# Output bias added to x by GpSimd instead of by two extra matmuls per block

## Chip, cores and metric

One Trainium2 chip (trn2), eight cores, one sequence of the batch on each; all cores run the same program on their own data and exchange nothing. The time is that of the slowest core, in microseconds on the device. Before: 2028.34 us, the median of three runs (2024.27 to 2031.74).

## What is computed

A hybrid encoder block on x of 4096 x 1024 per core. Cut to what matters here:

```python
h = rms_norm(x, g_mix)
u = h @ w_in + b_in                          # GLU | q | k | v
y_conv = silu(layer_norm(depthwise_conv(glu(u)) ...))
y_attn = windowed_gqa_with_sink(rope(q), rope(k), v)
x = x + (concat(y_conv, y_attn) @ w_out + b_out)     # the bias b_out
x = x + memory_cross_attention(rms_norm(x), rms_norm(mem))
x = x + swiglu(rms_norm(x), w_gate, w_up, w_down)
return rms_norm(x, g_final)
```

## The kernel before, in words

The program is written as a list of operations. Each is given to an engine with what it reads and writes (`Sched.op`, L63); `arrange` (L101) then orders the whole list with a cost for each operation: at each step the operation that comes first in the program among those ready takes its engine. `finalize` adds the semaphore waits. Each engine runs its operations in that fixed order, so one that waits holds up all behind it. For GpSimd ("pool") these are one-column powers for the norms (L392 and L1009) and the issue of transfers that convert weights from f32 to bf16.

The first 450 us (stages A and conv) project all blocks of 128 tokens and run the convolution; their results go to scratch in HBM. The rest runs over 8 groups of four blocks. `p_chains(g)` is the front half of a group: LayerNorm and swish of the conv half (`ln_stat`, `ln_z`, `ln_tr`, `ln_silu` with L1042, L1044 and L1046), attention per block (`scores` L1071 and L1075, `smax` L1089, `exps` L1105, `den2` with eight L1125), output projection (`out_proj`), cross attention (`mem_chain`) and the norm before the feed forward. `f_steps(g)` is the feed forward, mostly matmuls of L365 and L1430, whose results VectorE takes from PSUM with L1401, L1407 and L1441. The front half of group g+1 is interleaved with the feed forward of group g, and with `final_steps(g-1)`: the last norm (L386, L392, L1349) and the stores of the output.

The residual x of a block lies in one of two sets of four f32 tiles, `xres[g % 2]`. `xload(t)` (L995) loads x of block t into its tile with a transfer on the SP queue; from group 2 on it is placed behind the store of the block that held the tile. `out_proj` calls `proj` (L1179) with `bias` true: the first of nine matmuls for each half of 512 columns multiplies `ones_pad`, which has ones in row 0 and zeros below, with `bout_pad`, which has b_out in row 0 and zeros below. The sum in PSUM is added to x by VectorE in `resid` (L1196). The tile `bout_pad` is cleared by VectorE (L471) and its row 0 is loaded (L478) on GpSimd's queue. PSUM tiles are handed out from lists, `bank_f` for the feed forward and `bank_p` for the front half; a matmul into a tile waits until the last reader of it is done. `conv_win` (L444) shares each conversion of w_in among VectorE (640 columns, L451), ScalarE and GpSimd (576 columns, L455).

Of the kernel before, what the change touches and what calls it, by code (L numbers as in the profile page):

```python
# [8 lines left out]
ALU = mybir.AluOpType  # L9

P = 128
# [222 lines left out]
def build_program():  # L234
    nc = bass.Bass("TRN2", target_bir_lowering=False)
    sc = Sched(nc)

    def dram_in(name, shape, dt=F32):
        return nc.dram_tensor(name, list(shape), dt, kind="ExternalInput").ap()
# [12 lines left out]
    b_out_d = dram_in("b_out", [D])  # L252
# [21 lines left out]
    def sb(name, shape, dt):  # L274
        return nc.alloc_sbuf_tensor(name, list(shape), dt)

    ident = sb("ident", [P, P], BF16)
    ones_pad = sb("ones_pad", [P, P], BF16)
    bout_pad = sb("bout_pad", [P, D], BF16)
# [15 lines left out]
    cb2 = Buf()  # L295
# [4 lines left out]
    def view(off, nkb, dt, shape):  # L300
        ap = arena[:, int(off * 512):int((off + nkb) * 512)]
        if dt == F32:
            ap = ap.bitcast(F32)
        n = 1
        for s_ in shape:
            n *= s_
        return fit(ap[:, 0:n], shape)
# [4 lines left out]
    def fresh(off, nkb):  # L312
        a = Atom()
        for b_ in atoms[int(off * 2):int((off + nkb) * 2)]:
            a.r.extend(b_.w)
            a.r.extend(b_.r)
        a.r = sorted(set(a.r), key=lambda z: z.n)
        return Buf([a])
# [21 lines left out]
    def bank_p():  # L340
        return free_p.pop(0)
# [7 lines left out]
    def dma(e, out, in_, reads, writes, sem, after=()):  # L349
        eng = {"sp": nc.sync, "act": nc.scalar, "pool": nc.gpsimd}[e]  # L350
        n = 1
        for s_ in in_.shape:
            n *= s_
        n *= 2 if in_.dtype == BF16 else 4
        return sc.op(e, lambda: eng.dma_start(out=out, in_=in_), reads=reads, writes=writes, dma=sem, nbytes=n, after=after)  # L355
# [112 lines left out]
    sc.op("dve", lambda: nc.vector.memset(mhalf[:], -0.5), writes=[cb2])  # L468
    sc.op("dve", lambda: nc.vector.memset(ones_pad[:], 0.0), writes=[cb2])
    sc.op("dve", lambda: nc.vector.memset(ones_pad[0:1, :], 1.0), writes=[cb2])  # L470
    sc.op("dve", lambda: nc.vector.memset(bout_pad[:], 0.0), writes=[cb2])  # L471
    sc.op("dve", lambda: nc.vector.memset(bpad, 0.0), writes=[bpad_b])
    sc.op("dve", lambda: nc.vector.memset(zt, 0.0), writes=[zt_b])
    i2 = dma("pool", mask[:], mask_d, [], [], csem2)
    bisem = DmaSem(nc, "bi")
    dma("pool", bpad[0:1, :], b_in_d.unsqueeze(0), [], [bpad_b], bisem)
    bosem = DmaSem(nc, "bo")
    dma("pool", bout_pad[0:1, :], b_out_d.unsqueeze(0), [], [cb2], bosem)  # L478
    id_b = Buf()
    id_b.atoms[0].w = (i1, i2)  # L480
    cb.atoms[0].w = (c1, c2)
# [281 lines left out]
    for e in range(8):  # L763
# [3 lines left out]
        for c0 in range(0, 64, 12):  # L767
# [3 lines left out]
            def f(e=e, c0=c0, n=n, bk=bk, ta=ta):  # L771
                ins = None
                for k in range(n):
# [3 lines left out]
            o = sc.op("pe", f, reads=[tb_] + [v_[1] for v_ in vws], writes=[bkb], cost=0.1 * n)  # L777
# [5 lines left out]
                  reads=[bkb, gfin_b], writes=[yb], cost=0.1 + 0.05 * n)  # L783
# [11 lines left out]
    def mk(off, nkb, dt, *shape):  # L795
        return view(off, nkb, dt, shape), fresh(off, nkb)
# [4 lines left out]
    WK, _ = mk(137, 16, BF16, KC, D)  # L801
    WK_b = [fresh(137 + 2 * k, 2) for k in range(KC)]
    VW = view(153, 16, BF16, (KC, D))
    VW_b = [reg(153 + 2 * k, 2, BF16, D)[1] for k in range(KC)]
    flags = {}

    def note(*key):
        flags[key] = flags.get(key, 0) + 1

    WO = view(121, 16, BF16, (KC, D))  # L810
    WO_b = reg(121, 16, BF16, D)[1]
# [112 lines left out]
    ymixT = view(169, 8, BF16, (KC, T))  # L924
    ymc_b = [fresh(169 + c, 1) for c in range(4)]
    yma_b = [fresh(173, 4) for _ in range(4)]
# [56 lines left out]
    def p_chains(g, last_f=None):  # L983
        chains = []
        xs = xres[g % 2]
# [9 lines left out]
        def xload(t):  # L995
            def f():
                b = 4 * g + t
                dma("sp", xs[t][0], x_d[b * P:(b + 1) * P, :], [], [xs[t][1]], xres_sem[g % 2][t])
                note("x", g, t)
            return f  # L1000

# [174 lines left out]
            add(t0 + 12.6, pv, banks_free(1))  # L1176
            add(t0 + 13.4, pv_ev)

        def proj(t, weights, wbufs, lhs, lhsb, bias):  # L1179
            out = []  # L1180
            for u in range(2):
                bk, bkb = bank_p()
                pairs = [(lhs(k), weights[:, k, u * 512:(u + 1) * 512]) for k in range(KC)]
                rd = list(lhsb) + list(wbufs)
                if bias:
                    pairs = [(ones_pad[:], bout_pad[:, u * 512:(u + 1) * 512])] + pairs
                    rd = rd + [cb2]
                sc.op("pe", mm_group(bk[:], pairs), reads=rd, writes=[bkb], cost=pe_cost(len(pairs), 512))
                out.append((bk, bkb))
            return out  # L1190
# [9 lines left out]
        def out_proj(t, t0):  # L1200
            st = {}

            def a():
                st["b"] = proj(t, WO, [WO_b], lambda k: ymixT[:, k, t * P:(t + 1) * P], ymc_b + [yma_b[t]], True)

            def b():
                resid(t, st["b"])
            add(t0, a, banks_free(2), seen("ln", g), seen("wo"))
            add(t0 + 1.8, b, seen("x", g, t))
# [35 lines left out]
        def mem_chain(t, t0):  # L1245
            st = {}
            ha, hb = hTm[t % 2]
            pa, pb = Pm[t % 2]
            pta, ptb = PmT[t % 2]
# [6 lines left out]
            norm_chain(t, t0 - 4, ev_m, lambda: flags.get(("att", g), 0) >= 4 and (t < 2 or flags.get(("mc", g, t - 2), 0) >= 1))  # L1256

            def s_mm():
                st["s"] = proj(t, WK, WK_b, lambda k: ha[:, k, :], [hb], False)

            def s_max():
                for u in range(2):
# [27 lines left out]
                give_p(bk, bkb)  # L1290

            def o_mm():
                st["o"] = proj(t, VW, VW_b, lambda k: pta[:, k, :], [ptb], False)
                note("mc", g, t)

            def o_ev():
# [262 lines left out]
```

How the kernel before makes its waits and increments, by code:

```python
    def finalize(self):  # L136
# [58 lines left out]
        cnt = {e: 0 for e in self.ENG}  # L195
        for o in self.ops:
            if o.dma is None and o.signal:
                cnt[o.e] += 1
                rank[(o.e, o.idx)] = cnt[o.e]
        nw = 0
        for o in self.ops:
            eng = self.eng[o.e]
            for k, v in o.waits:
                if isinstance(k, str):
                    eng.wait_ge(self.sems[k], rank[(k, v)])
                else:
                    eng.wait_ge(k.sem, v)
                nw += 1
            ins = o.fn()
            if o.dma is not None:
                ins.then_inc(o.dma.sem, 16)
            elif o.signal:
                ins.then_inc(self.sems[o.e], 1)
        self.stats = dict(n_ops=len(self.ops), n_waits=nw, signals=cnt, end=max(o.start for o in self.ops))
# [1 line left out]
    def final_wait(self, e, dsems):  # L216
        eng = self.eng[e]
        for ds in dsems:
            if ds.count > 0:
                eng.wait_ge(ds.sem, ds.count)
```

## Time and profile before

| | |
|---|---|
| profiled execution | 2019.87 us |
| its span on the slowest core (core 3) | 2018.6 us |
| spans of the eight cores | 1975.7 to 2018.6 us |
| granted TensorE clock, mean of core 3 | 0.959 |
| TensorE, VectorE, ScalarE, GpSimd busy | 92%, 55%, 43%, 6% |
| instructions on GpSimd | 206 |

The profile is of one execution. PE is TensorE's matmuls, PEld its weight loads, DVE VectorE, ACT ScalarE, POOL GpSimd, SP the SyncE queue that issues most loads. L365 is line 365 of the kernel; it is a helper, and stands for most matmul groups. "arena" is the one large SBUF tensor in which nearly all tiles are views. Matmuls are pipelined: a row's duration is longer than the distance to the next one, and it is the distance that counts.

### The profile page before, as it was taken

To read this page: it belongs to the slowest core of one execution; us is meant where nothing else is said; L and a number is where in the kernel's file an instruction comes from. 1 tells how busy PE (TensorE), PEld (TensorE's weight loads), DVE (VectorE), ACT (ScalarE), POOL (GpSimd) and SP (SyncE) were. 2 spreads that over 40 slices of the span, in tenths; PEclk is the share of its full clock that TensorE was granted. 3 is DMA by queue.
4 is the path that set the end of the run, shared out by engine and by line. 5 is a ranking of instruction groups with operands and counts; after the bars stand their busy time and mean duration, and the time that the engine had idled before them with its cause. 6 is when DMAs were issued, how large, how long until landed. Compare 5 with 4: busy or idle time off the path is not lost.

```text
span 2018.6 us, 34398 instructions; the slowest of 8 cores (1975.7 to 2018.6 us)
## 1 busy us (share of the span) xinstructions
PE 1854.5 (92%) x11516; PEld 970.1 (48%) x11516; DVE 1110.2 (55%) x2430; ACT 872.1 (43%) x1761; POOL 122.4 (6%) x206
## 2 busy tenths in 40 slices
PE   3969998975775999999999999999999999999997
PEld 2535556842332544454454455445544544544443
DVE  4746665755353545754764485457547644754432
ACT  4534543543532453544455344535444553545210
POOL 2100000001001000000000000000000000000000
PEclk7989998977897999999999999999999999999999
DMA  8999864677079415331622353163316324521532
GB/s 246 185 205 196 203 157 153 150 202 227 0 128 151 142 48 200 133 120 58 230 105 82 124 205 118 50 213 131 108 58 230 105 80 131 178 100 58 188 141 100
DMA packets 80934, 284.71 MB, mean 141 GB/s; under 512 B 7159, under 2 KB 38777, under 8 KB 62872
## 3 DMA queue, kind: packets, MB, share of 16 engines
q1 hardware_dynamic: 73592, 237.74, 36.4%
q0 software_dynamic: 2560, 27.99, 9.8%
q10 hardware_dynamic: 4608, 16.78, 2.0%
q8 instruction: 95, 1.56, 0.3%
q14 instruction: 79, 0.65, 0.1%
HBM read 273.16 MB, written 65.10 MB: 168 GB/s over the span
## 4 chain that ended last, share of the span: by engine, by line
PE 76%; DMA 9%; issue 5%; DVE 5%; ACT 2%; SPq 1%; DVEq 0%; ACTq 0%; POOL 0%; POOLq 0%
PE bank L365 51%; PE bank L1430 15%; PE bank L373 5%; PE bank L774 2%; DMA arena<-s_y 2%; PE bank L1071 2%; SPq L355 1%; DMA arena<-w_in 1%; DMA arena<-s_gu 1%; DMA arena<-s_out 1%; ACT arena L386 1%; PE bank L1075 1%; DMA arena<-x 1%; DMA s_q<-arena 1%; PE bank L508 1%
## 5 line engine op out<-in xcount | busy, mean ns | idle before, releaser
L365 PE MATMUL bank<-arena 128*128 128x512 bf16 (+1 forms) x5724 | 1287.5, 377 | 23.4 <-ACT arena L1289 4.9
L365 PEld LDWEIGHTS bank<-arena 128*128 128x128 bf16 x5724 | 555.3, 99 | 629.8 <-issue 62.2
L1430 PE MATMUL bank<-arena 128*128 128x512 bf16 x1408 | 323.2, 379 | 0.6 <-DVE arena L1441 0.6
L386 ACT ACTIVATE arena<-arena 128x1024 bf16<-128x1024 f32 x130 | 137.2, 1056 | 309.8 <-DVE arena L1441 148.6
L1105 ACT ACTIVATE arena<-bank,asm 128x384 bf16<-128x384 f32 (+1 forms) x256 | 146.6, 573 | 157.4 <-DVE asm L1093 120.0
L1430 PEld LDWEIGHTS bank<-arena 128*128 128x128 bf16 x1408 | 133.7, 98 | 149.7 <-issue 7.5
L1396 ACT ACTIVATE arena<-bank 128x512 f32<-128x512 f32 x176 | 105.1, 597 | 214.1 <-PE bank L365 211.0
L373 PE MATMUL bank<-ident,arena 128*128 128x128 bf16 x2080 | 157.4, 224 | 39.1 <-DVE arena L632 15.3
L373 PEld LDWEIGHTS bank<-ident,arena 128*128 128x128 bf16 x2080 | 136.8, 100 | 85.4 <-issue 52.3
L1089 DVE TENSOR_REDUCE asm<-bank 128x1 f32<-128x384 f32 (+1 forms) x256 | 139.7, 546 | 57.2 <-PE bank L1075 49.8
L392 POOL TENSOR_TENSOR stat<-stat,mhalf 128x1 f32<-128x1 f32 x130 | 79.2, 610 | 1390.3 <-DVE stat L390 1354.9
L1401 DVE SCALAR_TENSOR_TENSOR arena<-arena,bank 128x512 f32<-128x512 f32 x176 | 119.6, 683 | 78.3 <-ACT arena L1396 77.7
L1196 DVE TENSOR_TENSOR arena<-bank,arena 128x512 f32<-128x512 f32 x128 | 88.3, 690 | 119.4 <-PE bank L365 117.8
L396 ACT ACTIVATE arena<-arena,stat 128x1024 bf16<-128x1024 f32 x98 | 112.4, 1147 | 88.4 <-POOL stat L392 88.0
L1407 DVE SCALAR_TENSOR_TENSOR arena<-arena,bank 128x512 bf16<-128x512 f32 x176 | 120.1, 685 | 38.3 <-PE bank L365 36.0
L1071 PE MATMUL bank<-arena 128*128 128x384 bf16 (+1 forms) x256 | 82.2, 333 | 48.3 <-ACT arena L1105 15.9
L1135 ACT COPY arena<-bank 128x1024 bf16<-128x1024 bf16 x94 | 90.2, 1019 | 51.2 <-PE bank L373 51.1
L1441 DVE TENSOR_TENSOR arena<-bank,arena 128x512 f32<-128x512 f32 x64 | 39.8, 684 | 120.5 <-PE bank L1430 120.5
L1125 DVE TENSOR_SCALAR arena<-arena,asm 128x384 bf16<-128x384 bf16 (+1 forms) x256 | 80.6, 315 | 12.1 <-DVE arena L1125 0.5
L1264 DVE TENSOR_REDUCE msm<-bank 128x2 f32<-128x512 f32 x64 | 44.3, 692 | 64.6 <-PE bank L365 64.4
L1272 ACT ACTIVATE arena<-bank,msm 128x256 bf16<-128x256 f32 x128 | 60.7, 474 | 29.9 <-DVE msm L1267 20.3
L1309 DVE TENSOR_TENSOR arena<-bank,vecs_sb 128x1024 bf16<-128x1024 bf16 x32 | 39.1, 1222 | 60.0 <-PE bank L373 60.0
(85 smaller groups left out, 1286.2 us busy)
## 6 DMA issues: line engine op xcount, KB each, us to landing
arena<-s_gu SPq DMA_DIRECT2D x88, 1024.0 KB, 6.0
arena<-x SPq DMA_DIRECT2D x64, 512.0 KB, 8.2
arena<-s_wd SPq DMA_DIRECT2D x32, 1024.0 KB, 4.9
out<-arena ACTq DMA_DIRECT2D x32, 512.0 KB, 3.7
arena<-s_wd SPq DMA_DIRECT2D x16, 768.0 KB, 4.6
s_gu<-w_gate_up POOLq DMA_DIRECT2D x11, 1024.0 KB, 10.2
s_mem<-w_memory POOLq DMA_DIRECT2D x8, 1024.0 KB, 13.6
arena<-s_mem SPq DMA_DIRECT2D x8, 1024.0 KB, 7.8
```

Of the source, the lines that this page charges most:

```text
L365: ins = nc.tensor.matmul(out_ap, l, r, start=(k == 0), stop=(k == n - 1))
L373: ins = nc.tensor.transpose(o, i_, ident[:])
L386: sc.op("act", lambda: nc.scalar.activation(junk, src, AF.Square, accum_out=st[:, 0:1]), reads=[srcb], writes=[junkb, stb], cost=1.26)
L396: sc.op("act", lambda: nc.scalar.activation(dst, src, AF.Copy, scale=st[:, 2:3]), reads=[srcb, stb], writes=[dstb], cost=1.16)
L1071: ins = nc.tensor.matmul(bk[:, w0:w1], qT[:, pp, t * P:(t + 1) * P], kz[:, h2, t * P + w0:t * P + w1], start=True, stop=False)
L1089: sc.op("dve", lambda bk=bk, h2=h2: nc.vector.tensor_reduce(a[:, 0, 2 * pp + h2:2 * pp + h2 + 1], bk[:, w0:w1], mybir.AxisListType.X, ALU. ...
L1105: sc.op("act", lambda bk=bk, hh=hh: nc.scalar.activation(Pt[:, hh, w0:w1], bk[:, w0:w1], AF.Exp, bias=a[:, 1, hh:hh + 1], scale=0.125, acc ...
L1135: sc.op("act", lambda: nc.scalar.copy(PTt[k], pst), reads=[bkb], writes=[PTt_b[k]], cost=1.02)
L1396: sc.op("act", lambda: nc.scalar.activation(ta, bk[:], AF.Tanh, scale=0.5), reads=[bkb], writes=[tb])
L1401: sc.op("dve", lambda: nc.vector.scalar_tensor_tensor(ta, ta, 1.0, bk[:], ALU.add, ALU.mult), reads=[bkb], writes=[tb])
L1407: sc.op("dve", lambda: nc.vector.scalar_tensor_tensor(actT[:, c, :], ta, 0.5, bk[:], ALU.mult, ALU.mult), reads=[bkb, tb], writes=[actT_b[c]])
L1430: sc.op("pe", lambda t=t, bk=bk: nc.tensor.matmul(bk[:], actT[:, c, t * P:(t + 1) * P], w3[:, c - c0, :], start=(c == 0), stop=(c == NFC - ...
```

## The change

The zeroing of `bout_pad` goes, and its load brings b_out to all 128 partitions, with a handle of its own (`bo_b`). Behind every load of an x block GpSimd adds the bias tile to it in place. `proj` has no bias branch any more, so each half of the output projection has eight matmuls instead of nine. The `cost=2.2` is what the planner reckons for the add.

```diff
-    sc.op("dve", lambda: nc.vector.memset(bout_pad[:], 0.0), writes=[cb2])
+    bo_b = Buf()
...
-    dma("pool", bout_pad[0:1, :], b_out_d.unsqueeze(0), [], [cb2], bosem)
+    dma("pool", bout_pad[:], b_out_d.partition_broadcast(P), [], [bo_b], bosem)
...
                 dma("sp", xs[t][0], x_d[b * P:(b + 1) * P, :], [], [xs[t][1]], xres_sem[g % 2][t])
+                sc.op("pool", lambda: nc.gpsimd.tensor_tensor(xs[t][0], xs[t][0], bout_pad[:], ALU.add), reads=[bo_b], writes=[xs[t][1]], cost=2.2)
                 note("x", g, t)
...
-        def proj(t, weights, wbufs, lhs, lhsb, bias):
+        def proj(t, weights, wbufs, lhs, lhsb):
...
-                if bias:
-                    pairs = [(ones_pad[:], bout_pad[:, u * 512:(u + 1) * 512])] + pairs
-                    rd = rd + [cb2]
...
-                st["b"] = proj(t, WO, [WO_b], lambda k: ymixT[:, k, t * P:(t + 1) * P], ymc_b + [yma_b[t]], True)
+                st["b"] = proj(t, WO, [WO_b], lambda k: ymixT[:, k, t * P:(t + 1) * P], ymc_b + [yma_b[t]])
```

## Rows read from the trace of the kernel before

**Rows 1.** The page's first part: busy time, share of span, instructions.
```profile
PE 1854.5 (92%) x11516; PEld 970.1 (48%) x11516; DVE 1110.2 (55%) x2430; ACT 872.1 (43%) x1761; POOL 122.4 (6%) x206
```

**Rows 2.** Busy time by stretch of core 3; the first line names the columns.
```profile
core 3: us, PE busy (x) PEld busy (x) DVE busy (x) ACT busy (x) POOL busy (x), PEclk, DMA share, GB/s
...
780.00:2018.60 1238.60, 1218.74 (x6863) 600.57 (x6861) 684.43 (x1492) 537.52 (x1101) 62.82 (x100) 1.00 0.38 130
```

**Rows 3.** Timeline of PE, 1003 to 1006 us: start, duration, instruction, count.
```profile
1003.36 0.38 PE L365 MATMUL bank<-bout_pad,ones_pad 128*128 128x512 bf16 x1
1003.58 1.89 PE L365 MATMUL bank<-arena 128*128 128x512 bf16 x8
1005.30 0.38 PE L365 MATMUL bank<-bout_pad,ones_pad 128*128 128x512 bf16 x1
```

**Rows 4.** The chain that ended last, 430 to 700 us: start, us, what.
```profile
485.36 17.82 PE bank L365 x72
...
591.64 23.68 DMA arena<-s_gu
```

**Rows 5.** Timelines of DVE and POOL, 20 to 29 us.
```profile
21.08 0.49 DVE L451 CAST arena<-arena 128x640 bf16<-128x640 f32 x1 [3.52 <-DMA arena<-w_in]
...
27.59 0.67 POOL L455 CAST arena<-arena 128x576 bf16<-128x576 f32 x1 [1.71 <-DMA arena<-w_in]
27.66 0.94 DVE L451 CAST arena<-arena 128x640 bf16<-128x640 f32 x1
```

**Rows 6.** Timelines of DVE and POOL, 972 to 976 us.
```profile
973.66 1.28 DVE L1349 SCALAR_TENSOR_TENSOR arena<-arena,stat,gfin 128x1024 f32<-128x1024 f32 x1
973.74 1.61 POOL L392 TENSOR_TENSOR stat<-stat,mhalf 128x1 f32<-128x1 f32 x1 [0.34 <-DVE asm L1093]
```

**Rows 7.** Timeline of SP, 978 to 991 us, the four x loads.
```profile
978.70 0.54 SPq L355 DMA_DIRECT2D arena<-x  x1
979.52 0.33 SPq L355 DMA_DIRECT2D arena<-x  x1
989.32 0.33 SPq L355 DMA_DIRECT2D arena<-x  x1
990.50 0.33 SPq L355 DMA_DIRECT2D arena<-x  x1
```

**Rows 8.** DMA issues at those four times, then g_final's: KB, us to landing.
```profile
arena<-x SPq DMA_DIRECT2D x1, 512.0 KB, 7.9
arena<-x SPq DMA_DIRECT2D x1, 512.0 KB, 9.9
arena<-x SPq DMA_DIRECT2D x1, 512.0 KB, 3.8
arena<-x SPq DMA_DIRECT2D x1, 512.0 KB, 6.5
...
gfin<-g_final SPq DMA_DIRECT2D x1, 512.0 KB, 10.4
```

**Rows 9.** Timeline of DVE, 986 to 995 us.
```profile
986.87 0.16 DVE L1121 TENSOR_TENSOR asm<-asm 128x8 f32<-128x8 f32 x1
...
988.40 0.31 DVE L1125 TENSOR_SCALAR arena<-arena,asm 128x384 bf16<-128x384 bf16 x1
...
990.25 0.31 DVE L1125 TENSOR_SCALAR arena<-arena,asm 128x384 bf16<-128x384 bf16 x1
...
992.02 0.32 DVE L1125 TENSOR_SCALAR arena<-arena,asm 128x384 bf16<-128x384 bf16 x1
...
993.42 0.81 DVE L1044 TENSOR_SCALAR arena<-bank,vech 128x512 f32<-128x512 bf16 x1 [0.25 <-ACT arena L1042]
```

**Rows 10.** Who waited for whom, 780 to 2018 us: total, times, longest.
```profile
PE bank L1071 <- DVE arena L1044: 4.2, 6, 0.7
```

**Rows 11.** Timelines of POOL and DVE, 1003 to 1008 us.
```profile
1003.18 0.55 POOL L1009 TENSOR_TENSOR bnst<-bnst,mhalf 128x1 f32<-128x1 f32 x1 [25.02 <-DVE bnst L1008]
...
1006.02 0.68 DVE L1196 TENSOR_TENSOR arena<-bank,arena 128x512 f32<-128x512 f32 x1
```

More of the change, by code:

```diff
@@ L1258, in s_mm @@
             def s_mm():
-                st["s"] = proj(t, WK, WK_b, lambda k: ha[:, k, :], [hb], False)
+                st["s"] = proj(t, WK, WK_b, lambda k: ha[:, k, :], [hb])
             def s_max():
@@ L1292, in o_mm @@
             def o_mm():
-                st["o"] = proj(t, VW, VW_b, lambda k: pta[:, k, :], [ptb], False)
+                st["o"] = proj(t, VW, VW_b, lambda k: pta[:, k, :], [ptb])
                 note("mc", g, t)
```

## Prediction, before the changed kernel was run

> **What bounds the kernel now.** Start with the busy shares: TensorE works 92% of the span, GpSimd 6% [rows 1]. The table by stretch splits this in two: up to 780 us TensorE has pauses; from there to the end it is busy 1218.7 of 1238.6 us at the full granted clock [rows 2]. In that part group follows group every 185 us, and a microsecond taken from TensorE is a microsecond of the end, unless it comes back as a wait; equally, whatever makes TensorE wait is paid in full, since it has no idle time later to make it up. So the question is not whether GpSimd has room (it has), but whether its new work delays something that TensorE waits for. The list of waits names the only regular one: six times, once for each of the last six groups, a score matmul (L1071) waits 0.7 us for a VectorE instruction of L1044 [rows 10], which frees the PSUM bank of a transpose. At this place VectorE sets the pace: in the timeline it works without a pause for some 7 us before it, alternating L1125 (scaling of the softmax), L1044 and L1046 (swish of the conv half) [rows 9].
>
> All times are of the profiled execution, 2019.87 us with a span of 2018.6. The median of the three timed runs is 2028.34; I add the difference worked out below to the median.
>
> **What goes.** Per block two matmuls of 512 columns, 64 in all. One starts at 1003.36 and the next matmul at 1003.58; the eight behind it reach to 1005.30, 1.72 us or 0.215 each [rows 3]. For the six groups after 780 us: 48 x 0.215 = 10.3 us, all on the path. Group 0: eight of them lie in an unbroken run of 72 matmuls that took 17.82 us, 0.2475 each, so 2.0 us [rows 4]. Group 1 is projected in the stage in which the chain runs through a load that waits for its converted weights (23.7 us) [rows 4]; its eight are worth 0 to 1.8 us, I take 1, since half of that stage is transfers. Sum 13.3 us. The weight loads belonging to them overlap matmuls and are worth nothing more. VectorE's memset of the bias tile goes too; it lay in a stretch where VectorE was waiting for the first loads: nothing.
>
> **The bias load.** It becomes a broadcast to 128 partitions, 512 KB read where 2 KB were, on GpSimd's queue at about 4.7 us. The nearest row, the broadcast of g_final of the same size, took 10.4 us to land [rows 8]. It is not needed before the 400th microsecond, but shares the DMA engines with the first constants, on which the weight loads wait. The quickest x load, of the same size, took 3.8 us from issue to landing, latency included [rows 8]; that is the upper end, and 0 the lower, if it fills a gap. It is early and small beside the weights, so I take 1 us.
>
> **The added GpSimd instruction.** 32 times 128x1024 f32 plus bf16 to f32. No row shows it. The nearest one is GpSimd's cast of 576 elements, 0.67 us when undisturbed [rows 5]. Scaled to 1024 elements with one input that is 1.2 us, with two inputs read one after the other 2.4. It has two inputs, and a part of the 0.67 doesn't grow with size, so I take 2.2 us; ends 1.2 and 2.4. By itself it is 32 x 2.2 = 70 us on an engine that is idle, and nothing.
>
> The Trainium skill (GPSIMD Engine Reference, "Elementwise: side-by-side cycle accounting") gives 4497 ns for an add of 2048 fp32 elements, so as an estimate 2.25 us for 1024, and advises against putting two-input elementwise work there. With it the sum below would differ by under 2 us.
>
> **What it does to VectorE.** The rows show that the two engines exclude each other. GpSimd's cast began at 27.59; VectorE's cast of 640 elements began 0.07 us later and took 0.94 us, where the one at 21.08 took 0.49: it stood still for 0.45 us, until GpSimd was nearly done [rows 5]. The other way round a power of one element per partition took 1.61 us, where another took 0.55 [rows 6, 11], when VectorE's L1349, which reads two SBUF tensors, began just ahead of it. So the add will hold back VectorE's fast SBUF-to-SBUF instructions (L1125) and those with two SBUF inputs (L1121, L1046), for what is left of its 2.2 us, and L1044 and others that read PSUM not.
>
> The Trainium skill (SBUF — State Buffer, "Who interferes with whom") draws this line: the port pair is an exclusive lock for a whole instruction, taken by VectorE in its 2-port modes or with two SBUF inputs, while an instruction with one SBUF input outside them is free. By that rule, the trace agrees for the cast and for L1349; for L1125 under a long add no row shows it.
>
> Where do the adds fall? Each waits for its x block. In the group at 978 us the loads are issued at 978.70, 979.52, 989.32 and 990.50 [rows 7] and land 7.9, 9.9, 3.8 and 6.5 us later [rows 8]: 986.6, 989.4, 993.1, 997.0. GpSimd has nothing else until 1003.18 [rows 11], so each add starts at once. That is just the stretch in which VectorE sets the pace. Worked through, "late" being VectorE's delay against its own times [rows 9]:
> - add 1, 986.6 to 988.8: L1121 (986.87) waits for it: late 1.9.
> - add 2, ready 989.4, lets one L1125 pass, 989.6 to 991.8: the L1125 of 988.40 waits: late 3.4.
> - add 3, 993.1 to 995.3: VectorE is in L1044, which is free; the L1125 of 990.25 waits: late 5.1.
> - add 4, 997.0 to 999.2: the L1125 of 992.02 waits: late 7.2.
>
> The L1044 of 993.42, for which TensorE waits, is then 7.2 us late, and TensorE's pause grows from 0.7 to 7.9 us. With an add of 1.2 us the same working gives 2.5 us (the fourth comes after), with 2.4 us 8. The six groups have the same order of x loads and of VectorE instructions and the same 0.7 us wait [rows 10], so 6 x 7.2 = 43 us, between 15 and 48. In groups 0 and 1 the x blocks land where TensorE later waits for weight transfers anyway: I take 0 there.
>
> **Waits moved.** L1196, the residual add, now waits for GpSimd in place of the DMA. Its first one starts at 1006.02 [rows 11], 19 us after its x landed and 4 us behind the end of the fourth add by the working above: hidden; should that cover go, the cost is what is left of an add, at most 2.2 us a group. Queued behind a waiting add on GpSimd are the powers of the LayerNorm, which come behind it, and in the first two groups the issues of the weight conversions; if one stood for a late x there, its transfer would start some us later, within the 0 to 2 us that I leave open. The order of all queues is made by a planner in the kernel whose costs change with the edit, so places can shift; it knows nothing of the exclusion, and the x loads still follow the output stores. I allow 6 us either way for it.
>
> **Sum.** -13.3 + 1 + 43 = +30.7 us on the profiled execution; rounded to +30 on the median: 2058. Ends: -13.3 + 0 + 15 = +2 (2030) and -12 + 3.8 + 48 = +40 (2068); with the planner's 6 us 2024 to 2074.
>
> **Rivals.**
> - The exclusion costs nothing: the saving stays. It does so if the adds run before 986.9 or behind 994.4, or if L1125 isn't held up by them. For it: nowhere does a row show L1125 stretched (but GpSimd ran nothing long beside it). Against: the landings above, and the casts. From an add late by over 8 us on, or with no exclusion, the time is 2028.3 - 13.3 + 1 = 2016, faster.
> - A short hold: the add takes 1.2 us, or lets VectorE in between its reads. Then 15 us come back against 13 saved: 2030, no change that can be measured.
> - More is lost than one chain: after the pause VectorE and ScalarE stay behind, more score matmuls wait (L1093 and L1196 release some now), or the powers come late: 10 us or so more, 2070 to 2085.
> - The bias matmuls do go, by the diff; that the edit doesn't do what it says is excluded.
>
> **How the numbers follow.** Main case 0.60, no cost from the exclusion 0.17, short hold 0.15, more lost 0.08. Under about 0.5% (10 us) a measurement of this kernel can't be told from no change. Slower: 0.60 + 0.08 + 0.02 of the short hold = 0.70; same 0.13; faster 0.17. The range 2022 to 2078 leaves out the faster case and the top of the last one, together 0.2.
>
> **What would show it.** In the changed profile: GpSimd busy up by 32 adds of about 2.2 us, to some 190 us, their count 32; VectorE busy up by about 35 us or more, in L1121, L1125 (now 0.32 us each) and L1046, whose means rise; TensorE's wait on L1044 about 7 us, six times; TensorE's matmul count down by 64, and the chain through the group showing VectorE lines. If L1125 keeps its 0.32 us, the exclusion is wrong; if it is stretched and TensorE doesn't wait, the place of the adds is; if the adds take 1.2 us, their price is. Wrong altogether it would be if the planner put the x loads or the swish elsewhere.

## The result, and the profile after

The changed kernel is slower: its time over that of the kernel before is 1.0201 [1.0169, 1.0233]. Its profiled execution took 2068.6 us, with a span of 2067.4 us on core 4, where the kernel before had 2019.87 and 2018.6. By the ratio the median goes from 2028 to 2069 us: about 41 us more, where the prediction had 30 more. All ratios here compare executions in the usual, faster state: two of the four timed executions of the changed kernel (2324.98 and 2336.31 us) were in a slower one, in which the cores of one die show a lower clock, and are left out.

The page's first part, as [rows 1]:

```profile
PE 1834.1 (89%) x11259; PEld 969.7 (47%) x11452; DVE 1153.2 (56%) x2429; ACT 873.2 (42%) x1761; POOL 189.9 (9%) x238
```

GpSimd has 32 instructions and 67.5 us more, TensorE 64 weight loads less (some of its matmul records are missing from this trace, so its 11259 can't be compared), and VectorE has one instruction less and yet 43 us more busy time. Where that time lies is told by the costliest groups of instructions (engine, operation, tiles, count | busy us, mean ns of one | idle time before them and who ended it):

```profile
L1126 DVE TENSOR_SCALAR arena<-arena,asm 128x384 bf16<-128x384 bf16 (+1 forms) x256 | 113.3, 443 | 12.7 <-DVE arena L1126 0.9 <-DVE asm L1124 0.3
L999 POOL TENSOR_TENSOR arena<-arena,bout_pad 128x1024 f32<-128x1024 f32 x32 | 69.2, 2168 | 102.5 <-DMA arena<-x 102.3
L1047 DVE SCALAR_TENSOR_TENSOR arena<-arena 128x512 bf16<-128x512 f32 x32 | 29.4, 923 | 0.2
```

The new line numbers are one or two off those of before: L1126 is the L1125 of [rows 9], which took 0.31 us there, L1045 is L1044, L1047 is L1046, L1072 is L1071, L1194 is L1196. L999 is the add. Each add starts when its x has landed (102.3 of 102.5 us of its engine's idle time end with that transfer).

Who waited for whom on TensorE from 760 us on, as [rows 10]: total, times, longest.

```profile
PE bank L1072 <- DVE arena L1045: 38.6, 6, 7.7
PE bank L373 <- DVE arena L1126: 2.6, 2, 1.6
```

The wait of 4.2 us in six has become 38.6, and it is the same one. What happens in one group is to be seen in the timelines of one stretch. GpSimd:

```profile
1195.87 4.77 POOL L999 TENSOR_TENSOR arena<-arena,bout_pad 128x1024 f32<-128x1024 f32 x2 [10.19 <-DMA arena<-x]
1200.94 2.12 POOL L999 TENSOR_TENSOR arena<-arena,bout_pad 128x1024 f32<-128x1024 f32 x1 [0.29 <-DMA arena<-x]
1204.82 2.12 POOL L999 TENSOR_TENSOR arena<-arena,bout_pad 128x1024 f32<-128x1024 f32 x1 [1.76 <-DMA arena<-x]
```

VectorE beside it:

```profile
1196.04 2.62 DVE L1047 SCALAR_TENSOR_TENSOR arena<-arena 128x512 bf16<-128x512 f32 x1
1198.58 2.18 DVE L1126 TENSOR_SCALAR arena<-arena,asm 128x384 bf16<-128x384 bf16 x1
1200.69 0.80 DVE L1045 TENSOR_SCALAR arena<-bank,vech 128x512 f32<-128x512 bf16 x1
1201.41 1.77 DVE L1126 TENSOR_SCALAR arena<-arena,asm 128x384 bf16<-128x384 bf16 x1
1203.10 0.68 DVE L1047 SCALAR_TENSOR_TENSOR arena<-arena 128x512 bf16<-128x512 f32 x1
...
1204.88 2.61 DVE L1047 SCALAR_TENSOR_TENSOR arena<-arena 128x512 bf16<-128x512 f32 x1
...
1207.64 0.80 DVE L1045 TENSOR_SCALAR arena<-bank,vech 128x512 f32<-128x512 bf16 x1
```

Four instructions are held, each until about the end of the add that runs beside it: L1047 takes 2.62 and 2.61 us in place of 0.68, L1126 2.18 and 1.77 in place of 0.31. That is 1.94 + 1.93 + 1.87 + 1.46 = 7.2 us. The L1045 of 1200.69, which reads PSUM, runs beside the adds with its usual 0.80. TensorE in the same stretch:

```profile
1208.59 0.48 PE L1072 MATMUL bank<-arena 128*128 128x384 bf16 x1 [7.73 <-DVE arena L1045]
1208.86 0.42 PE L1076 MATMUL bank<-mask,ident 128*128 128x128 bf16 x2
1209.08 2.76 PE L373 MATMUL bank<-ident,arena 128*128 128x128 bf16 x24
```

It waits 7.73 us in place of 0.70, so the 7.2 us of VectorE come out at TensorE as 7.0. And the 24 transposes behind the wait take 2.76 us, where in the kernel before they took 1.50:

```profile
994.65 1.50 PE L373 MATMUL bank<-ident,arena 128*128 128x128 bf16 x24
```

The same place one group earlier shows why, first in TensorE's timeline, then in the table by stretch (columns as in [rows 2], PEclk is the granted clock):

```profile
1014.02 0.34 PE L1072 MATMUL bank<-arena 128*128 128x384 bf16 x1 [4.61 <-DVE arena L1045]
...
1016.15 2.72 PE L373 MATMUL bank<-ident,arena 128*128 128x128 bf16 x24 [1.58 <-DVE arena L1126]
```

```profile
1009.40:1014.00 4.60, 0.02 (x1) 0.01 (x1) 4.60 (x8) 0.78 (x1) 2.35 (x2) 1.00 0.67 278
1014.00:1016.00 2.00, 0.55 (x3) 0.24 (x3) 2.00 (x2) 0.00 (x0) 1.89 (x1) 0.55 0.99 288
1016.00:1018.00 2.00, 1.85 (x18) 1.88 (x19) 2.00 (x5) 0.74 (x1) 0.00 (x0) 0.50 0.70 250
1018.00:1020.00 2.00, 1.78 (x12) 1.16 (x11) 2.00 (x4) 2.00 (x3) 0.00 (x0) 0.50 0.59 246
1020.00:1022.00 2.00, 2.00 (x10) 0.90 (x9) 0.20 (x1) 0.28 (x2) 0.00 (x0) 0.74 0.00 0
1022.00:1024.00 2.00, 2.00 (x13) 0.99 (x11) 1.89 (x4) 0.42 (x1) 0.00 (x0) 1.00 0.00 0
```

TensorE stands still for 4.6 us. Its first score matmul behind that still takes 0.34 us, the usual time; it then waits another 1.58 us, and from about there it has half the clock, the lower of its two levels (1.2 of 2.4 GHz), for some 6 us. This is a cost that the prediction did not have.

To set a sum beside the forecast, two numbers are taken from every trace, each a mean over the eight cores: the time at which the first of the six waits on L1045 (L1044 before) ends, and the distance from the first to the last of them divided by five, the length of a group.

| kernel | mean wait | first wait ends | length of a group |
|---|---|---|---|
| before | 0.70 | 792.1 | 185.33 |
| changed | 6.87 | 810.6 | 191.35 |
| changed, second profile (e0) | 6.58 | 800.9 | 191.03 |
| e1, no adds | 0.70 | 799.4 | 183.99 |
| e2, adds late | 0.70 | 791.2 | 183.77 |
| e3, half adds | 2.49 | 797.5 | 185.85 |
| e4, adds in four | 3.09 | 798.9 | 186.91 |
| e6, adds beside the bias matmuls | 6.79 | 799.1 | 193.29 |
| e7, e2 and bias load late | 0.70 | 785.9 | 183.88 |
| e8, only the delay | 7.36 | 799.7 | 193.22 |
| e9, one conversion moved | 6.66 | 799.7 | 191.18 |
| e10, e7 with VectorE | 0.70 | 786.4 | 182.88 |
| e11, VectorE at the change's place | 1.35 | 818.0 | 184.68 |

A group is thus 6.0 us longer after the change. What is left behind the last wait stayed the same: 285.7 us on core 3 before, 285.3 after.

### The profile page after: what moved, and what is told of

Read it like the earlier page. It is cut to its first block, busy times and chain, and to the rows that moved or that the text cites. A ratio compares the mean times of both kernels' runs of the same rounds, so it can differ in the third digit from the quotient of the medians.

```text
span 2067.4 us, 34116 instructions; the slowest of 8 cores (2033.5 to 2067.4 us)
## 1 busy us (share of the span) xinstructions
PE 1834.1 (89%) x11259; PEld 969.7 (47%) x11452; DVE 1153.2 (56%) x2429; ACT 873.2 (42%) x1761; POOL 189.9 (9%) x238
## 4 chain that ended last, share of the span: by engine, by line
PE 72%; DMA 13%; issue 6%; DVE 5%; ACT 2%; SPq 1%; POOL 0%; DVEq 0%; ACTq 0%; another core or an unknown queue 0%; POOLq 0%
PE bank L365 47%; PE bank L1428 14%; PE bank L373 5%; DMA s_v<-arena 3%; PE bank L774 2%; DMA arena<-s_y 1%; PE bank L1072 1%; SPq L355 1%; DMA arena<-w_in 1%; DMA arena<-s_gu 1%; DMA arena<-s_out 1%; DVE arena L1126 1%; PE bank L508 1%; DMA s_y<-arena 1%; DMA arena<-x 1%
## 5 line engine op out<-in xcount | busy, mean ns | idle before, releaser
L365 PE MATMUL bank<-arena 128*128 128x512 bf16 (+1 forms) x5575 | 1261.3, 376 | 44.7 <-POOL arena L455 7.2
L365 PEld LDWEIGHTS bank<-arena 128*128 128x128 bf16 x5724 | 554.4, 99 | 634.8 <-issue 68.3
L1428 PEld LDWEIGHTS bank<-arena 128*128 128x128 bf16 x1408 | 133.6, 98 | 149.7 <-issue 7.5
L373 PE MATMUL bank<-ident,arena 128*128 128x128 bf16 x2080 | 163.9, 230 | 41.2 <-ACT arena L396 12.5
L373 PEld LDWEIGHTS bank<-ident,arena 128*128 128x128 bf16 x2080 | 143.1, 103 | 88.9 <-issue 57.1
L1090 DVE TENSOR_REDUCE asm<-bank 128x1 f32<-128x384 f32 (+1 forms) x256 | 139.7, 546 | 65.3 <-PE bank L1076 58.3
L1072 PE MATMUL bank<-arena 128*128 128x384 bf16 (+1 forms) x256 | 81.1, 330 | 94.2 <-DVE arena L1045 38.6
L1194 DVE TENSOR_TENSOR arena<-bank,arena 128x512 f32<-128x512 f32 x128 | 88.4, 691 | 114.7 <-PE bank L365 111.1
L1126 DVE TENSOR_SCALAR arena<-arena,asm 128x384 bf16<-128x384 bf16 (+1 forms) x256 | 113.3, 443 | 12.7 <-DVE arena L1126 0.9
L1072 PEld LDWEIGHTS bank<-arena 128*128 128x128 bf16 x256 | 25.1, 98 | 119.3 <-issue 104.5
L999 POOL TENSOR_TENSOR arena<-arena,bout_pad 128x1024 f32<-128x1024 f32 x32 | 69.2, 2168 | 102.5 <-DMA arena<-x 102.3
## 6 DMA issues: line engine op xcount, KB each, us to landing
arena<-x SPq DMA_DIRECT2D x64, 512.0 KB, 10.8
```

The costliest lines, as they stand in the source:

```text
L365: ins = nc.tensor.matmul(out_ap, l, r, start=(k == 0), stop=(k == n - 1))
L373: ins = nc.tensor.transpose(o, i_, ident[:])
L1072: ins = nc.tensor.matmul(bk[:, w0:w1], qT[:, pp, t * P:(t + 1) * P], kz[:, h2, t * P + w0:t * P + w1], start=True, stop=False)
L1090: sc.op("dve", lambda bk=bk, h2=h2: nc.vector.tensor_reduce(a[:, 0, 2 * pp + h2:2 * pp + h2 + 1], bk[:, w0:w1], mybir.AxisListType.X, ALU. ...
L1126: sc.op("dve", lambda hh=hh: nc.vector.tensor_scalar(Pt[:, hh, w0:w1], Pt[:, hh, w0:w1], a[:, 4, hh:hh + 1], None, ALU.mult), reads=[b_[4] ...
L1428: sc.op("pe", lambda t=t, bk=bk: nc.tensor.matmul(bk[:], actT[:, c, t * P:(t + 1) * P], w3[:, c - c0, :], start=(c == 0), stop=(c == NFC - ...
```

## Experiments

Two theories. A: GpSimd's add and VectorE's instructions on SBUF exclude each other, and since the adds fall on the stretch where VectorE sets the pace, TensorE waits that much longer, with a clock penalty on top. B: something else came with the edit (the order of the planner, the bias load, memory traffic, an add that waits for its x), and the exclusion is beside the point.

**The changed kernel once more (e0).** No edit.

> The changed kernel itself, unaltered, timed beside the other three and the kernel before on one chip. Ratio 1.020, as measured first.

Measured 1.0229 [1.0183, 1.0275], waits of 6.58 us. The result stands. The length of a group repeats within 0.3 us, but the stretch up to the first wait is 9.7 us shorter than in the first profile, with the same program. So differences of some microseconds in that stretch, between single profiles, prove nothing.

**No adds (e1).** In the changed kernel:

```diff
-                sc.op("pool", lambda: nc.gpsimd.tensor_tensor(xs[t][0], xs[t][0], bout_pad[:], ALU.add), ...)
```

> The changed kernel without the 32 GpSimd adds; the output bias is left out of the computation. The broadcast load and the eight-matmul projections stay. Theory (the adds hold VectorE up, VectorE holds TensorE up): the waits on L1045 fall back to 0.7 us, and the time is before less the 13 us saved plus 1 to 2 us of the larger load at the start: about 2016 us, ratio 0.994. Rival (the loss comes from the new order of the queues or from the start, not from the adds): the time stays above that of before, 2030 to 2068.

Measured 0.9971 [0.9934, 1.0009], and of the waits:

```profile
PE bank L1071 <- DVE arena L1044: 4.2, 6, 0.7
```

So without the adds the wait is exactly that of before, and a group is 183.99 us long, 1.3 shorter than before. The ratio is above the 0.994 expected: of the 13 us that the matmuls were to be worth, 8 lie in the six groups, and in the first part none came back (below).

**Half an add (e3).** 512 of 1024 columns:

```diff
-... nc.gpsimd.tensor_tensor(xs[t][0], xs[t][0], bout_pad[:], ALU.add) ...
+... nc.gpsimd.tensor_tensor(xs[t][0][:, 0:512], xs[t][0][:, 0:512], bout_pad[:, 0:512], ALU.add) ...
```

> The changed kernel with adds over 512 of the 1024 columns, so the bias is added to half of the output's columns only. GpSimd's time for an add falls from 2.13 to about 1.1 us. Theory (what counts is how long one add holds VectorE's instruction, times the adds that fall before the last L1045): delay 2.5 us a group in place of 7, no fall of the granted clock or a short one: 2018 to 2030 us, ratio 0.995 to 1.001. Rival (a fixed cost for each add, or the wait on x's landing): little less than the changed kernel, 2050 or more.

Measured 1.0046 [1.0012, 1.0081]. The add:

```profile
L999 POOL TENSOR_TENSOR arena<-arena,bout_pad 128x512 f32<-128x512 f32 x32 | 38.3, 1197 | 120.7 <-DMA arena<-x 109.9 <-DVE bnst L1007 10.6
```

1.20 us for 512 columns against 2.17 for 1024: extended to no columns, about 0.25 us don't grow with the size. The mean wait is 2.49 us, as expected, and the group is 1.86 us longer than without adds, of which the wait makes 1.79. The ratio lies above the 0.995 to 1.001 expected: the first wait ends 5.4 us later than before, of which the longer wait itself makes about 2.

**The same work in four pieces (e4).** Four adds of 256 columns each, with a quarter of the cost to the planner:

```diff
+                for c in range(4):
+                    cs = slice(256 * c, 256 * c + 256)
+                    sc.op("pool", lambda cs=cs: nc.gpsimd.tensor_tensor(xs[t][0][:, cs], xs[t][0][:, cs], bout_pad[:, cs], ALU.add), ..., cost=0.55)
```

> The changed kernel with each add of 1024 columns split into four of 256, one behind the other, GpSimd's work being the same or somewhat longer. Theory (an add holds VectorE's instruction until the add has ended, and in the gap between two adds VectorE gets its turn): an instruction of VectorE waits for one quarter, some 0.6 us, in place of up to 2.1, and L1044 runs beside the next quarter; VectorE is late by some 4 us a group in place of 7 and TensorE's wait on L1045 is about 4 us. Time 2035 to 2050, ratio 1.005 to 1.012. Rival (bandwidth is shared, so only the total of GpSimd's work counts): as the changed kernel, 1.018 to 1.022.

Measured 1.007 [1.0051, 1.009]. The adds, then TensorE's wait:

```profile
L1001 POOL TENSOR_TENSOR arena<-arena,bout_pad 128x256 f32<-128x256 f32 x128 | 93.3, 742 | 86.3 <-DMA arena<-x 74.9 <-POOL arena L1001 1.3
...
PE bank L1074 <- DVE arena L1047: 18.8, 6, 3.5
```

More work in all for GpSimd (93.3 us against 69.2), and less than half the wait: 3.1 in place of 6.9 us. VectorE gets in after every piece. What counts is how long one instruction keeps the other out, not how long GpSimd is busy; this tells the exclusion from a general slowing of memory, which would have grown with the 93 us.

**Adds later (e2).** They get an order behind the last L1047 of the group and the last L1126 of its first block (`tail`), and are emitted there:

```diff
+        def xadd(t):
+            def f():
+                sc.op("pool", lambda: nc.gpsimd.tensor_tensor(xs[t][0], xs[t][0], bout_pad[:], ALU.add), ..., cost=2.2, after=list(tail))
...
+        for t in range(4):
+            add(15.0 + 3 * t, xadd(t), seen("xl", g, t), seen("ln", g), seen("den", g))
```

> The changed kernel with each add made to wait for the last swish instruction of its group (L1047) and the last softmax scaling of its first block (L1126), so that the four adds of a group run behind the stretch in which VectorE sets the pace. Same work, other place. Theory: TensorE's wait on L1045 falls back to about 0.7 us, the adds (4 x 2.1 us) end before or about at the first residual add some 11 us later; 2016 to 2022 us, ratio 0.994 to 0.997. If the last adds still reach the first residual add or the powers of the LayerNorm, 1 to 2 us a group come back: up to 2030. Rival (an add costs VectorE its 2.1 us wherever it runs): 2050 to 2068.

Measured 0.9943 [0.9904, 0.9981]. GpSimd in the group near 990 us, and TensorE's wait:

```profile
991.01 8.39 POOL L1005 TENSOR_TENSOR arena<-arena,bout_pad 128x1024 f32<-128x1024 f32 x4 [16.77 <-DVE arena L1053]
```

```profile
PE bank L1079 <- DVE arena L1051: 4.2, 6, 0.7
```

The same four adds, 8.4 us in a row, a few microseconds later, and the wait is 0.7 again. With e1 and e4 this settles that the loss in the six groups is the adds' place and length, not their presence.

**Only the delay (e8).** Nothing on GpSimd, and the bias matmuls of the kernel before. In groups 2 to 7 two reductions of a PSUM tile, whose results nobody uses, stand inside the operation of L1044, so that the planner sees the old cost and every queue keeps its order:

```diff
+                    if g >= 2:
+                        nc.vector.tensor_reduce(junk[:, 0:2], pst, mybir.AxisListType.X, ALU.max)
+                        nc.vector.tensor_reduce(junk[:, 2:3], src, mybir.AxisListType.X, ALU.max)
```

> The kernel before, its queues in exactly the order of before, nothing added on GpSimd; in groups 2 to 7 two VectorE instructions (maxima over the PSUM tile, about 1.7 us together) stand ahead of each L1044, which makes its fourth about 6.8 us late. Theory A (late VectorE is paid by TensorE one to one): 6 x 6.8 = 41 us, ratio 1.020. Theory B (and TensorE's clock falls to its lower level behind the pause, about 2 us a group more): 6 x 8.8 = 53 us, ratio 1.026, granted clock 0.50 for some 5 to 7 us behind each pause. Rival (the loss needs GpSimd, by something other than the time VectorE stands still): under 1.010.

Measured 1.0248 [1.0223, 1.0272], between the 1.020 of theory A and the 1.026 of theory B, and with the lower clock of B. The reductions, the wait, and TensorE's clock behind one of the pauses:

```profile
L1048 DVE TENSOR_REDUCE junk<-bank 128x2 f32<-128x1024 bf16 x24 | 29.3, 1222 | 0.0
L1049 DVE TENSOR_REDUCE junk<-bank 128x1 f32<-128x512 bf16 x24 | 16.4, 682 | 0.0
```

```profile
PE bank L1078 <- DVE arena L1050: 44.3, 6, 7.6
```

```profile
1010.00:1012.00 2.00, 1.48 (x13) 1.34 (x14) 2.00 (x5) 0.00 (x0) 0.00 (x0) 0.50 1.03 294
1012.00:1014.00 2.00, 2.00 (x19) 1.72 (x18) 2.00 (x4) 1.84 (x3) 0.00 (x0) 0.50 0.63 258
1014.00:1016.00 2.00, 2.00 (x7) 0.78 (x6) 0.79 (x2) 1.00 (x2) 0.00 (x0) 0.59 0.16 66
1016.00:1018.00 2.00, 2.00 (x15) 1.06 (x13) 1.14 (x3) 0.60 (x1) 0.00 (x0) 1.00 0.00 0
```

A group is 7.89 us longer than before, of which the wait makes 6.66. The other 1.2 us is the lower clock behind the pause: TensorE has no more work than before, and yet its busy time in a group (by the table by stretch, mean of eight cores) is 185.3 us in place of 183.5. So VectorE's lateness alone, with no bias load and no adds, costs what the adds cost and a little more (a group 7.89 us longer, against 7.36 in the changed kernel set beside e1); nothing else of the edit is needed for the six groups.

**A delay that the planner could see through (e5).** The same delay as two copies of each L1044 as operations of their own:

```diff
+                for _ in range(2 if g >= 2 else 0):
+                    sc.op("dve", lambda: nc.vector.tensor_scalar(wa, src, vech[:, cc:cc + 1], vech[:, 4 + cc:5 + cc], ALU.mult, ALU.add),
+                          reads=[bkb, cb2], writes=[wb], cost=0.01)
```

> The kernel before, with nothing on GpSimd, but in groups 2 to 7 each L1044 is followed by two copies of itself (0.72 us each from start to start, eight copies a group, 5.8 us). It separates what a VectorE delay costs from who causes it. Six of the eight lie before the fourth L1044 ends, at which TensorE waits, and the two behind it do not delay that but the matmuls after it. Theory A (a delay of VectorE is paid one to one by TensorE): 6 x 5.8 = 35 us less what hides, so 2055 to 2063 us. Theory B (and after a pause of 4 us or more TensorE runs at the lower clock level for some us): 2 us a group more, 2065 to 2075, with a granted clock below 1.00 behind each pause. Rival (VectorE has slack): under 2040.

Measured 1.0101 [1.007, 1.0132], a miss. The planner put work of the feed forward between the copies and moved the scores, so that the list of waits looks otherwise:

```profile
PE bank L373 <- DVE arena L1128: 10.6, 6, 2.0
```

No pause is longer than 2.0 us. It tells nothing about the theory, since the order was not held; e8 holds it.

**The adds with the bias matmuls kept (e6).** In the kernel before, the bias load as in the change, the adds, and the matmuls stay:

```diff
+    dma("pool", bout_pad[:], b_out_d.partition_broadcast(P), [], [bo_b], bosem)
...
+                sc.op("pool", lambda: nc.gpsimd.tensor_tensor(xs[t][0], xs[t][0], bout_pad[:], ALU.add), reads=[bo_b], writes=[xs[t][1]], cost=2.2)
```

> The kernel before with the adds and the broadcast load, and the bias matmuls kept, so the bias goes in twice. It separates what is added from what is taken away. Theory: all of the loss and none of the gain: waits of 7 us on L1044, a pause-induced lower clock, 2 us at the start: +50 to +55 us, ratio 1.025 to 1.027, unless the planner's order changes as well. Rival (the adds only hurt in the new order): under 1.020.

Measured 1.0252 [1.0224, 1.028]. A group is 193.29 us long, 1.9 more than in the changed kernel, for eight matmuls that the prediction put at 1.7. So the two halves of the change add up: the saving is real, and the adds cost about four times as much.

**Bias load late too (e7).** As e2, and the load of `bout_pad` goes behind the last projection of stage A.

```diff
-    dma("pool", bout_pad[:], b_out_d.partition_broadcast(P), [], [bo_b], bosem)
...
+    dma("pool", bout_pad[:], b_out_d.partition_broadcast(P), [], [bo_b], bosem, [a_last[0]])
```

> The kernel with the late adds, and besides the broadcast load of the bias issued behind the last projection of stage A instead of with the first constants. Theory (the 512 KB of the broadcast hold up the first transfers: w_dw landed after 10.2 to 11.3 us in place of 8.1 to 9.3): the start is about 2 us earlier, w_dw lands after 8 to 9.3 us; ratio to before 0.992 to 0.994. Rival (the start is covered by later waits): no difference from the kernel with late adds alone, 0.994.

Measured 0.994 [0.9921, 0.996]. The chain at the start of the changed kernel and of this one (start, us, what):

```profile
3.47 11.29 DMA arena<-w_dw
```

```profile
3.47 8.75 DMA arena<-w_dw
```

It was 9.06 in the kernel before. These are single cores, and the cores of one profile differ by up to 2.6 us. On the mean of eight this load takes 10.8 us in the changed kernel and 10.6, 10.4 and 10.6 in e0, e1 and e2, against 9.1 in the kernel before and 8.9 in e7 and e10. The early load thus costs about 1.7 us of the first transfer. Against e2 (0.9943) the timing can't resolve it; in the profiles the first wait ends 5.3 us earlier, which is within what one program showed between two profiles (e0).

**The order of one conversion (e9).** In the kernel before, GpSimd issues the fourth conversion of the down weights behind the third LayerNorm power of group 2 (at 638 us in the profile), in the changed one ahead of it (625 us). Here it is put back:

```diff
+        if k == 24:
+            held.append(c_)
...
+                if g == 2 and t == 2:
+                    held[0].deps.add(p_)
```

> The changed kernel with one issue on GpSimd's queue put back to where it stands in the kernel before: the fourth conversion of w_down (s_wd, 1 MB) behind the third LayerNorm power of group 2 instead of ahead of it. All other queues keep the changed kernel's order. Theory (without the bias matmuls the planner issues this transfer some 15 us earlier, it shares the DMA engines with the load of s_y, which VectorE and then TensorE wait for around 640 us): the s_y load at 620 us takes 19 to 20 us in place of 24 to 26, the long waits of TensorE between 570 and 660 us fall by some 5 to 10 us, time 0.25 to 0.5% below the changed kernel, ratio to before 1.015 to 1.019. Rival (that stage is set by the conversions' total, or differs by chance): no change, 1.020 to 1.023.

Measured 1.0199 [1.0171, 1.0226] against 1.0201 and 1.0229 for the same kernel without it. The measured ratio lies just outside the expected 1.015 to 1.019, and the intervals overlap: that conversion is not shown to matter.

**VectorE does the late adds (e10).** As e7, with

```diff
-                sc.op("pool", lambda: nc.gpsimd.tensor_tensor(...), ..., cost=2.2, after=list(tail))
+                sc.op("dve", lambda: nc.vector.tensor_tensor(xs[t][0], xs[t][0], bout_pad[:], ALU.add), ..., cost=1.3, after=list(tail))
```

> The kernel with the late adds and the late broadcast, with the adds on VectorE instead of GpSimd: 1.1 to 1.3 us each (the 128x512 residual adds take 0.69, L1349 with 1024 columns 1.28), 4 a group, behind the last swish instruction. Theory (VectorE sets the pace only in the stretch before; behind it it has pauses): four adds make it late by 5 us right where the feed forward's PSUM tiles wait for it, so TensorE waits for 1 to 3 us a group: 2014 to 2030, ratio 0.996 to 1.004, worse than GpSimd at the same place (0.994). Rival (VectorE is the quicker engine and takes no lock): as good or better, 0.994 or less.

Measured 0.9913 [0.9889, 0.9937], 2004 us: the best of all, and faster than both kernels. I had expected 0.996 to 1.004, since VectorE is the busier engine. One of the adds, and the whole group of them:

```profile
987.12 1.21 DVE L1005 TENSOR_TENSOR arena<-arena,bout_pad 128x1024 f32<-128x1024 f32 x1
```

```profile
L1005 DVE TENSOR_TENSOR arena<-arena,bout_pad 128x1024 f32<-128x1024 f32 x32 | 38.7, 1214 | 3.2 <-DMA arena<-x 3.1
```

1.21 us each, spread by the planner between instructions of the feed forward. VectorE has pauses there, and a group is 182.88 us long on every core, 1.0 shorter than in e7 and 2.45 shorter than before. The waits tell the difference. In e7, whose adds are GpSimd's:

```profile
PE bank L1079 <- DVE arena L1166: 5.5, 5, 1.5
PE bank L1079 <- DVE arena L1051: 4.2, 6, 0.7
PE bank L1079 <- DVE arena L1204: 4.1, 12, 0.7
```

In e10:

```profile
PE bank L1079 <- DVE arena L1051: 4.2, 6, 0.7
PE bank L1079 <- DVE arena L1204: 1.3, 5, 0.5
```

With GpSimd's adds, 8.4 us in a row, TensorE waits up to 1.5 us for VectorE instructions behind them (L1166, and L1204 of the output projection); with VectorE's own these waits are nearly gone. The core shown is one of the slower in e7; on the mean of eight, all waits but the one on L1051 take 1.0 us a group in e7 and 0.4 in e10, 0.6 of the 1.0 us. That VectorE loses less by 1.21 us of its own time than by being kept out for 2.1 us fits this, but no run here separates it from where the planner put the adds.

The Trainium skill (GPSIMD Engine Reference, "Elementwise: side-by-side cycle accounting") gives a ratio of 1.96 between the two engines for a two-input add of 2048 fp32 elements and keeps "use DVE for elementwise" as the rule. By that rule, the traces agree: for 1024 columns, undisturbed, 2.12 against 1.21 us is 1.75, and the version on VectorE is the faster one.

**VectorE at the change's own place (e11).** The changed kernel, early bias load, the add right behind the load of x, but on VectorE:

```diff
-                sc.op("pool", lambda: nc.gpsimd.tensor_tensor(...), ..., cost=2.2)
+                sc.op("dve", lambda: nc.vector.tensor_tensor(...), ..., cost=1.3)
```

> The changed kernel with the add given to VectorE in its program place (right behind the load of x), planner's price 1.3 us, early bias load kept; nothing is left out. In VectorE's queue one of the four adds of a group now stands ahead of the L1045 that TensorE waits for, between L1122 and L1124, and the other three stand behind the chain between the reads of the feed forward. Theory A (GpSimd's adds cost through the exclusion; on VectorE only an add's own 1.21 us counts): the L1045 wait is 0.7 + 1.2 = about 2 us, six times, no stretched L1126 (mean 0.315 us), the clock stays at 1.00; from the run without adds (0.997) plus 6 x 1.2 us (0.0036) = 1.001, between 0.998 and 1.004. Theory B (an add so early costs because it waits for its x block, whichever engine does it, and everything behind it waits too): VectorE idles at L999 for the x transfer, 2 to 6 us a group, and the L1045 wait is 4 us or more: 1.008 to 1.018. If the kernel with late VectorE adds (0.9913) is good because of the engine and not because of the place, this one is at 0.992 to 0.996.

Measured 1.009 [1.0073, 1.0108], a miss of theory A and inside theory B's range, though not for B's reason in the six groups. In the six groups it is as theory A said: no L1126 is stretched, one add of a group stands ahead of the L1045 chain, the mean wait is 1.35 us, and a group is 184.68 us long, 0.7 more than without adds. But the first wait ends only at 818.0 us, over 30 us behind e10. The chain of waits between 380 and 680 us shows that VectorE's queue waits for x in the first two groups:

```profile
428.46 9.24 DMA arena<-x
...
467.63 21.31 DMA arena<-x
```

There the planner had put adds between reads of PSUM tiles (L887 and L1090), which then had to wait for the x blocks. So theory B is right for this kernel in groups 0 and 1, and the engine alone doesn't make e10 good; the place does as much.

On GpSimd the wait for x is cheaper, but not nothing: there the LayerNorm powers of the first groups stand behind it. In the changed kernel the chain passes through an x load near 440 us on four cores of eight (5.58 us on core 4), and in e0, e3, e4 and e6, which have the adds at the same place, on one to three. In the kernel before, in e1, e2, e8 and e9 it does so on none. In e6:

```profile
446.26 4.88 DMA arena<-x
451.27 1.08 POOL arena L999
```

It need not cost as much as it lasts, since e6 is at its first wait no later than e8, which has no adds.

## Why the prediction was right and where it was off

- **Direction and mechanism: right.** VectorE's instructions on SBUF stand still for the length of an add, L1045 goes with them and so does TensorE, six times. Without adds, with the adds later, and in pieces the wait shrinks as said (e1, e2, e4; half adds in e3); the delay without GpSimd gives the same loss (e8).
- **The price of the add: right.** 2.17 us on average, undisturbed 2.12, where I took 2.2 from bounds of 1.2 and 2.4.
- **Who is held: right, and wider than shown.** L1126, never seen stretched before, went from 0.31 to as much as 2.22 us on the core shown and L1047 from 0.68 to 2.62; L1045 kept its 0.80. VectorE's busy time grew by 43 us, where I had said 35 or more.
- **7.2 us a group: the right size.** The mean wait grew by 6.17 us (6.87 less 0.70), not by 7.2. The stretch at 1195 us is nearly the one worked, 7.2 us of stretched instructions. In others, such as the one at 1005 us with its wait of 4.61, an add falls on a free instruction and less is lost.
- **What was missing: the clock.** I had weighed a longer pause of TensorE as its length and no more. Against the kernel without adds a group is 7.36 us longer and the wait only 6.17: 1.2 us a group are not in the wait. They are not in other waits either, which take 0.8 us a group in place of 1.1; TensorE's busy time for the same matmuls is longer, 183.6 us in a group against 181.9 in e1 (mean of eight cores), and the rows show the lower clock there. The same remainder is 1.2 in e0 and e9, and, against the kernel before, 1.2 in e8 and 1.9 in e6. In e3, where the mean wait was 2.49 us, it is 0.1, in e4 (3.09) 0.5.
- **The saving: slightly over-sized.** 1.34 us a group by e1, 1.9 by e6, for 1.72 in the sum.
- **Together** a group became 6.0 us longer, where the sum had 7.2 - 1.72 = 5.5. Over six groups that is 36 instead of 33 us: the two errors, 1 us too much for the wait and 1.2 too little for the clock, nearly cancel. That the size fits so well is luck.
- **The first 800 us: the term that made 30 into 41.** The sum had +1 for the bias load and -3 for the matmuls of groups 0 and 1, together -2 us. Measured, and less the longer first wait, this stretch grew by 12.3 us in the profile of the result and by 2.9 in that of e0. Part is known: the bias load cost about 1.7 us at the start and not 1 (e7). The x blocks of groups 0 and 1, taken as 0, stand in the chain of half the cores (e11), at a price that no run isolates. The saving of 3 us is not seen, and e1, which has it, is 7.3 us later than before at that place; in e7 and e10, which have it and not the early load, the place comes 6.2 and 5.7 us earlier. A saving ahead of a wait for a transfer comes back only if the transfer comes sooner, and I had counted it in full for group 0 although the chain runs through weight transfers afterwards [rows 4]. That is an argument, not shown. The chain of the changed kernel there:

```profile
593.35 25.34 DMA arena<-s_gu
622.25 25.90 DMA arena<-s_y
```

  Waits of TensorE of 5 us and more that end between 560 and 660 us add up to 33.5 us a core (mean of eight) in the changed kernel, and to 30.4 in e0, 32.6 in e1, 29.2 in e3, 31.7 in e4 and 28.6 in e9. They are 25.9 before, and 26.3, 25.4, 25.7, 25.6, 24.5 and 26.0 in e2, e5, e6, e7, e8 and e10. (In e11, held up earlier, they are 23.3.) The cores of one profile differ by more than that, 14.6 to 30.7 before, but the two sets of means don't overlap in thirteen profiles, so chance is an unlikely cause. It is not the adds (e6 has them, e1 hasn't), nor the early bias load (e2 and e6 have it). The higher set is the kernels without the bias matmuls whose adds, if any, stand right behind the x load: it goes with the order that the planner makes of them. Which place of the order does it stays open; e9 put one piece back and remained in the higher set. The 6 us left to the planner were too few for it.
- **Two slips in the working, without effect.** The first L1196 stands 6.8 us behind the end of the fourth add (1006.02 less 999.2), not 4; from 780 us on no L1194 of the core shown waited for GpSimd, so "hidden" was right. And the trace lists the bias load with 256.0 KB and 9.9 us to landing, where I had 512 KB.
- **Rivals.** "The exclusion costs nothing" and "a short hold" fell with the stretched rows. "More is lost than one chain" came true in small: the clock, and the 2.6 us that TensorE waited for L1126 on the core shown.

## What to carry to other kernels

Ask of an idle engine not only what it has room for but what it locks: on the stretch where VectorE sets the pace, four GpSimd instructions of 2.17 us, 8.7 us in all, made a group 7.4 us longer, and moving them a few microseconds behind that stretch turned 2% slower into 0.6% faster. When work must run beside a busy engine, give it to the engine that does it fastest, place it where that engine has slack and its input is surely there, and keep early loads off the first transfers. Price a new pause of TensorE as its length plus what the clock takes behind it.

## What the runs showed of the hardware

- After a pause of 4.6 us TensorE had a granted clock of about 0.50 for some 6 us, and 24 transposes took 2.72 to 2.76 us in place of 1.50. Behind the pause of 7.73 us the clock was back after some 3.5 us. In e3 even a pause of 3.07 us did so:

```profile
1000.55 0.48 PE L1072 MATMUL bank<-arena 128*128 128x384 bf16 x1 [3.07 <-DVE arena L1045]
1001.04 2.77 PE L373 MATMUL bank<-ident,arena 128*128 128x128 bf16 x24
```

  while in e4 one of 3.04 us did not at once (its first score matmul kept 0.32 us, the granted clock was 1.00 from 1005 to 1007 us and 0.51 from 1007 to 1009), so no fixed length of a pause can be read from these runs. What the lower clock took was 1.6 us a group by TensorE's busy time, and 1.2 net, since other waits became shorter.
- GpSimd's add of f32 and bf16 to f32 took 2.12 us for 1024 columns, 1.20 for 512 and 0.74 for 256; VectorE's 1.21 for 1024.
- The lock is for a whole GpSimd instruction, and between two of them VectorE gets in: the same adds in four pieces took 35% more of GpSimd's time and more than halved the wait.
